# Inputs of a two-layer hybrid trunk stored as columns and tiles, and a bias table stored once per query

## The reference, cut to what matters

```
h = concatenate([meta, x], axis=1)
for layer in range(2):
    nw = norm_w[layer]
    f = swiglu(rms_norm(h, nw[0]), w_gate[layer, 0], w_up[layer, 0], w_down[layer, 0])
    h = h + 0.5 * rms_norm(f, nw[1])
    hn = rms_norm(h, nw[2])
    mix = even_mixer(hn, ...) if layer % 2 == 0 else odd_mixer(hn, ...)
    h = h + rms_norm(mix, nw[3])
    f = swiglu(rms_norm(h, nw[4]), w_gate[layer, 1], w_up[layer, 1], w_down[layer, 1])
    h = h + 0.5 * rms_norm(f, nw[5])
return h[:, 16:]
```

## Time and profile before

| | us |
|---|---|
| median of 3 runs | 2066.17 |
| lowest and highest of them | 2065.93 and 2068.43 |
| the profiled execution, its own time | 2064.44 |
| its span, first to last instruction | 2062.7 |

### The profile page before, as it was taken

How to read it: one execution, slowest core, us unless ns; L and a number is a source line. 1 busy time by engine, 2 the same in 40 slices (tenths; PEclk the granted TensorE clock), 3 DMA queues, 4 the chain that set the end, 5 groups by cost and what they waited for, 6 DMA issues and landing times.

```text
span 2062.7 us, 38830 instructions
## 1 busy us (share of the span) xinstructions
PE 2036.9 (99%) x16054; PEld 1960.1 (95%) x16054; DVE 1381.5 (67%) x2042; ACT 1021.4 (50%) x1751; POOL 102.6 (5%) x97
## 2 busy tenths in 40 slices
PE   8999999999999999999999999999999999999998
PEld 7999999998999999999999999999998789999887
DVE  6989831667485399988228998822663449998723
ACT  5655632446535465556225555622453456555612
POOL 0000000100052200000100000010000020000000
PEclk9999999999999999999999999999999999999999
DMA  4333342321110133333313333331322123333332
GB/s 133 99 103 103 105 127 77 87 73 52 42 32 12 52 103 98 107 105 105 113 50 102 88 107 104 103 112 53 95 81 69 42 67 97 103 109 110 110 96 78
DMA packets 329043, 180.64 MB, mean 88 GB/s; under 512 B 15849, under 2 KB 323344, under 8 KB 328878
## 3 DMA queue, kind: packets, MB, share of 16 engines
q1 hardware_dynamic: 327520, 175.30, 29.6%
q0 software_dynamic: 1024, 2.86, 0.6%
q10 hardware_dynamic: 334, 0.14, 0.0%
HBM read 176.16 MB, written 2.12 MB: 86 GB/s over the span
## 4 chain that ended last, share of the span: by engine, by line
PE 95%; DVE 3%; ACT 1%; DMA 0%; issue 0%; POOL 0%; SPq 0%; DVEq 0%; ACTq 0%
PE psum L1287 35%; PE psum L713 31%; PE psum L725 13%; PE psum L939 5%; PE psum L3172 1%; PE psum L3231 1%; DVE w_hl L569 1%; PE psum L2633 1%; PE psum L3730 1%; PE psum L2645 0%; DMA stage<-ffn_w_gate 0%; PE psum L3746 0%; PE psum L3741 0%; DVE acts L2002 0%; PE psum L816 0%; PE psum L792 0%
## 5 line engine op out<-in xcount | busy, mean ns | idle before, releaser
L1287 PE MATMUL psum<-seven_x,w_hl 128*128 128x264 f32 (+1 forms) x3456 | 438.3, 283 | 0.0
L569 DVE TENSOR_TENSOR w_hl<-stage,w_hl 128x1024 fp32r<-128x1024 f32 (+1 forms) x166 | 220.7, 1330 | 309.7 <-ACT w_hl L562 309.4
L1287 PEld LDWEIGHTS psum<-seven_x,w_hl 128*128 128x128 f32 x3456 | 425.0, 188 | 0.0
L713 PE MATMUL psum<-x_hl,w_hl 128*128 128x264 f32 (+1 forms) x2736 | 368.0, 293 | 2.2 <-DVE w_hl L569 1.9
L713 PEld LDWEIGHTS psum<-x_hl,w_hl 128*128 128x128 f32 x2736 | 348.5, 189 | 14.8 <-issue 5.5
L1287 PE MATMUL psum<-x_hl,w_hl 128*128 128x264 f32 (+1 forms) x2592 | 338.2, 284 | 0.0
L1287 PEld LDWEIGHTS psum<-x_hl,w_hl 128*128 128x128 f32 x2592 | 324.5, 188 | 0.0
L562 ACT ACTIVATE w_hl<-stage 128x1024 fp32r<-128x1024 f32 (+1 forms) x166 | 189.1, 1140 | 227.3 <-PE psum L713 71.5
L713 PE MATMUL psum<-acts,w_hl 128*128 128x264 f32 x2376 | 289.0, 284 | 0.0
L713 PEld LDWEIGHTS psum<-acts,w_hl 128*128 128x128 f32 x2376 | 288.7, 188 | 0.0
L725 PE MATMUL psum<-x_hl,w_hl 128*128 128x264 f32 (+1 forms) x1728 | 219.2, 286 | 0.6 <-DVE w_hl L569 0.4
(11 more groups left out here) (401 smaller groups left out, 2186.5 us busy)
## 6 DMA issues: line engine op xcount, KB each, us to landing
stage<-ffn_w_down SPq DMA_DIRECT2D x48, 704.0 KB, 4.7
stage<-ffn_w_gate SPq DMA_DIRECT2D x52, 512.0 KB, 3.8
stage<-ffn_w_up SPq DMA_DIRECT2D x52, 512.0 KB, 3.8
x_raw<-ffn_w_gate SPq DMA_DIRECT2D x32, 512.0 KB, 3.8
x_raw<-ffn_w_up SPq DMA_DIRECT2D x32, 512.0 KB, 3.8
stage<-odd_w_in SPq DMA_DIRECT2D x24, 512.0 KB, 3.8
stage<-ffn_w_down SPq DMA_DIRECT2D x22, 512.0 KB, 3.5
stage<-even_w_in SPq DMA_DIRECT2D x18, 512.0 KB, 3.8
```

The source lines that it names most:

```text
L569: dve.tensor_tensor(weights(core.w_hl[:, slot.ring, 1, :], *kind), weights(core.stage[:, slot.stage, :], *kind), weights(core.w_hl[:, slot ...
L713: op = pe.matmul(out, lhs, moving[:, moved, kt, t0:t0 + n], start=first and part + moved == 0, stop=last and part == 1)
L1287: op = pe.matmul(k.psum[:, bank, 0:w], k.w_hl[:, slot.ring, side, at:at + P], moving(moved, kt), start=start and kt + side + moved == 0, s ...
```

## The change

Three things are done, all with the layout of what lies in DRAM.

Tokens and channel vectors as columns. The host lays tokens (meta tokens ahead) out as `tokens`, partition by channel tile by token, and the norm weights and channel vectors as `channel_cols`, 128 by 151. SP loads the tokens straight into `h` in four pieces of two channel tiles, in this order: gate tile of group 0, pieces 0 and 1, up tile, pieces 2 and 3. ACT issues two loads, `norm_cols` and `vec_cols`; `ident` goes to POOL's list. All transposes of the start are gone, and with them L1388, L1402 in two pieces, L1410, L2255 and L2257. ACT and DVE start with the weights' split and then take the tokens piece by piece; both wait for both vector loads first.

Bias rows stored once per query. POOL stores `bias_row` 128 times, once for each query row of a block: 1024 pieces of 2800 bytes instead of 8. The read in the even mixer has a stride of one stored copy less one element, gives the queries in their order and lands in `bias`, `bias_near` and `bias_self` themselves. The ten matmuls and ten copies of slot 5 are gone, with the load of `flip`. ACT's wait for the store is gone; `bias_row` now lies where `acts_raw` keeps tile 16, and DVE waits for the store before it writes that tile in the first feed-forward. DVE, not PE, waits for the rows in the even mixer.

Weights by tiles. All weight tiles but those of the last step lie in DRAM in the order in which they land in SBUF, 4 KB (5.5 KB for `ffn_w_down`) in one piece for each partition. The query tiles are gathered on the host and come by one load each.

```diff
-CONST_LOADS = 11
-SCALAR_LOADS = 6
+TOKEN_PIECES = ((0, 1), (2, 3), (4, 5), (6, 7))
+BIAS_TILE = 16
+CONST_LOADS = 8
+SCALAR_LOADS = 2
...
+        self.bias_row = self.at("bias_row", [QH, V_ALL], low + BIAS_TILE * tile)
...
+def load_tokens(core, sp, a, piece):
+    first, last = TOKEN_PIECES[piece][0], TOKEN_PIECES[piece][-1]
+    sp.dma_start(core.h[:, first:last + 1, :], a["tokens"][:, first:last + 1, :])\
+      .then_inc(core.tokens_in[piece], 16)
...
-            src = w[:, n * P:(n + 1) * P].rearrange("(k p) n -> p k n", p=P)
-            sp.dma_start(group_stage(core, n, side, slot), src)\
+            sp.dma_start(group_stage(core, n, side, slot), w[n])\
                 .then_inc(core.w_landed[slot.stage], 16)
+            if phase is core.phases[0] and n == 0:
+                load_tokens(core, sp, a, 2 * side)
+                load_tokens(core, sp, a, 2 * side + 1)
...
+    src = a[name][bass.ds(tile, 1)].rearrange("a p k n -> p (a k) n")
+    sp.dma_start(weights(dst, DT, P), src).then_inc(core.w_landed[slot.stage], 16)
...
+    def run(slot, piece):
+        slot.out_pair = slot.pair
+        if piece == 0:
             pe.wait_ge(k.w_lo, slot.count())
+        for kt in TOKEN_PIECES[piece]:
+            pe.wait_ge(k.x_lo, kt + 1)
+            op = products(k, pe, phase, slot, kt, kt, k.x_hl, kt == 0, kt == DT - 1)
         if kt == DT - 1:
             op.then_inc(k.slot_used, 1)
...
+    run(slots[0], 0)
     pe.wait_ge(k.consts_set, 5)
     pe.wait_ge(k.consts_in, 16 * (CONST_LOADS - SCALAR_LOADS))
...
+    run(slots[0], 1)
+    run(slots[1], 0)
+    run(slots[1], 1)
+    for piece in (2, 3):
+        for slot in slots:
+            run(slot, piece)
...
+    def piece(i):
+        act.wait_ge(k.tokens_in[i], 16)
+        for kt in TOKEN_PIECES[i]:
+            col = first.before.pre_col + kt
+            act.activation(k.x_hl[:, 0, kt, :], k.h[:, kt, :], ACT.Copy, scale=k.norm_cols[:, col:col + 1])\
+               .then_inc(k.x_hi, 1)
+        for kt in TOKEN_PIECES[i]:
+            act.activation(k.in_squares[:, kt, :], k.h[:, kt, :], ACT.Square).then_inc(k.sq_made, 1)
...
+    high(0)
+    act.wait_ge(k.norms_in, 16)
+    act.wait_ge(k.vectors_in, 16)
+    piece(0)
+    piece(1)
+    high(1)
+    piece(2)
+    piece(3)
+    high(2)
...
-    act.wait_ge(k.bias_stored, 16)
...
+    if phase is k.phases[0] and n == BIAS_TILE:
+        dve.wait_ge(k.bias_stored, 16)
...
+    low(0)
+    dve.wait_ge(k.norms_in, 16)
+    dve.wait_ge(k.vectors_in, 16)
+    piece(0)
+    piece(1)
+    low(1)
+    piece(2)
+    piece(3)
+    dve.wait_ge(k.sq_made, DT)
+    add_squares(DT // 2)
+    low(2)
...
-    pool.wait_ge(k.cols_ready, 4)
-    pool.dma_start(a["bias_scratch"], k.bias_row[0:QH, :]).then_inc(k.bias_stored, 16)
+    pool.wait_ge(k.cols_ready, 2)
+    copies = k.bias_row[0:QH, :].unsqueeze(1).broadcast_to([QH, P, V_ALL])
+    pool.dma_start(a["bias_scratch"].rearrange("p h v -> h p v"), copies).then_inc(k.bias_stored, 16)
...
-        return bass.AP(tensor, first, [[1, rows], [V_ALL, QH], [1, n]])
+        return bass.AP(tensor, first + rows - 1, [[QH * V_ALL - 1, rows], [V_ALL, QH], [1, n]])
...
+    pool.dma_start(e.bias[:, :, META:BANDS], skewed(V_BAND, P, 2 * P)).then_inc(e.rows_in, 16)
...
-        pe.wait_ge(e.rows_in, 80)
-        for j in range(BIAS_FLIPS):
-            if j >= len(FLIP_BANKS):
-                pe.wait_ge(e.bias_set, j - len(FLIP_BANKS) + 1)
...
-        pe.wait_ge(e.bias_set, BIAS_FLIPS)
         pe.wait_ge(e.v_rows_set, 3)
...
-        for j in range(BIAS_FLIPS):
-            bank = FLIP_BANKS[j % len(FLIP_BANKS)]
-            dve.wait_ge(e.bias_flip, j + 1)
...
+        dve.wait_ge(e.rows_in, 64)
         dve.memset(e.gates[:], 1.0).then_inc(e.gates_clear, 1)
```

More of the change, by code:

```diff
@@ L233, in count @@
             before["added"] += phase.early if self.split else DT - 1
-        if not self.split:
-            before["h"] += 2 * DT
         if self.pre_col is not None:
@@ L316, in linked @@
 def linked(steps):
-    queries = [s.slot0 for k, s in steps if k == "dense" and s.kind == "in" and s.layer == 0]
-    twice = [first + t for first in queries for t in range(QH // KVH)]
     for at, (kind, step) in enumerate(steps):
@@ L523, in landed @@
         first = self.base + RING * (self.i if self.peeled else 1)
-        twice = [g for g in self.twice if g <= first and g % 2 == self.stage]
-        return self.i * (16 * RING // 2) + 16 * (self.base // 2 + 1 + len(twice) - self.single)
+        return self.i * (16 * RING // 2) + 16 * (self.base // 2 + 1 - self.single)
 def walk(core, phase, engine, step, ahead=0, between=None, late=False):
@@ L674, in load_slot @@
     if phase.kind == "rows":
-        rows = a["ffn_w_down"][phase.layer, phase.ffn][bass.ds(slot.local * P, P), :]
+        rows = a["ffn_w_down_rows"][bass.ds(slot.local * P, P), :]
         sp.dma_start(dst[:, 0:D], rows).then_inc(core.w_landed[slot.stage], 16)
@@ L1039, in tensor_input @@
               stop=True).then_inc(k.cols_flip, 1)
-    for slot in slots:
-        run(slot, DT - 2)
-        run(slot, DT - 1)
+    run(slots[0], 1)
[4 more added lines that the diff above has]
+            run(slot, piece)
 def tensor_dense(core, pe, phase):
@@ L3957, in odd_vector, with tiles_of @@
         lo(kt)
+def tiles_of(array, count):
+    rows, cols = array.shape[-2], count * P
+    tiles = array[..., 0:cols].reshape(array.shape[:-2] + (rows // P, P, count, P))
+    return np.moveaxis(tiles, -2, -4).swapaxes(-3, -2)
 def laid_out(name, array):
+    if name == "ffn_w_gate" or name == "ffn_w_up":
+        return tiles_of(np.asarray(array), FT)
+    if name == "ffn_w_down":
+        tiles = tiles_of(np.asarray(array), DT)
+        tiles = tiles.reshape(tiles.shape[:-2] + (2, FH, P))
+        return np.moveaxis(tiles, -3, -4)
+    if name == "even_w_in":
+        whole = np.array(array[0])
+        heads = whole[:, 0:QH * HD].reshape(D, KVH, GRP, HD).transpose(0, 2, 1, 3)
+        whole[:, 0:QH * HD] = heads.reshape(D, QH * HD)
+        return tiles_of(whole, EVEN_TILES)
+    if name == "odd_w_in":
+        return tiles_of(np.asarray(array)[0], ODD_TILES)
+    if name == "odd_w_out":
+        return tiles_of(np.asarray(array)[0], DT)
     if name == "rel_bias_table" or name == "swa_sinks":
```

226 lines of the change are left out of this document (55 added, 171 removed).

## The result

The changed kernel takes 2085.09 us (median of 4 runs, 2085.00 to 2085.86); the kernel before, beside it, takes 2066.05. The ratio is 1.0094, with an interval from 1.0081 to 1.0106: slower by 19 us, where 13 us less were forecast. The profiled execution's span is 2084.1 us instead of 2062.7.

The account below looks back on a forecast made before the run. PE, busy 2036.9 of 2062.7 us, bounds the kernel; 9.3 us at the start plus 3.7 in slot 5, with 0 for weights and store, take 13.0 off 2066.17: 2053.2 us, range 2049.5 to 2059.

Parts of the forecast that it names:

- the room that the store takes on the DMA engines: Head, between 19 and 40 us: the store runs beside four to five weight tile loads; cost 0, upper bound 4 us.
- Rival (3): Head, 19 to 60 us: the store crowds out weight loads, giving back 4 us: 2057.2 us; chance 12%.
- The rule on the number of engines: Store of the bias rows: 8 DMA engines by the rule, some 15 us at half of peak, weight tiles waiting on these.
- The start: First two slots' 96 products: their end moves from 32.8 to 23.5 us, a gain of 9.3 us.
- S: Start: the moment when the first tokens can be scaled, taken as 6.5 us, range 5.9 to 8.
- 4.7 us after its first product: Start: PE works at half rate for about 4.7 us after its first product, charged as 2.35 us.
- The opposite reading: Start: slow time runs from PE's first instruction, lasts 10 us and costs 2.7 us more.
- the second rival: Start brings only half: vectors land at 7.9 us, slow stretch lasts 10 us; 2057.4 us; chance 15%.
- Slot 5: Even mixer's input projection: PE no longer waits for DVE's copies before the next score product; gain 3.7 us.
- The clock in the mixer: Two windows of 50 us from 500 us on: 3 us of work lost, other spacing may lose 1.5 more or less.
- The weights by tiles: Weight loads in pieces of 4 KB instead of 512 bytes: worth 0, bounds 0 and -0.5 us.
- rival (5): Wait before tile 16: a slow store holds DVE and PE; 68 us lost, 2121 us, at the upper bound; chance 2%.

Follow-up runs that it names:

- e13: Changed kernel, but the store reads 8 partitions of `h` lying 4 apart, 128 times each (bias values wrong): 2055.32 us.
- e4: Changed kernel with the bias rows stored once to DRAM, then copied 128 times within DRAM (the two-step kernel): 2050.35 us, ratio 0.9939 to the kernel before.
- e1: Changed kernel with the old bias path (one small store, ten matmuls and ten copies in slot 5): 2052.14 us, ratio 0.9949 to the kernel before.
- e5: e4 with the weights in DRAM in rows as the reference has them, query tiles still gathered on the host: 2053.92 us.
- e6: e4 with 26 matmuls of ones by ones into an unused PSUM bank ahead of PE's first product: 2049.54 us.
- e9: Changed kernel, but the store reads 8 partitions of `h` lying 2 apart, 128 times each (bias values wrong): 2060.75 us, timed once.
- e11: e4's text unchanged, timed again in more rounds against the kernel before: 2053.59 us, ratio 0.9951.
- e7: Changed kernel, but the store reads 16 neighbouring partitions of `h`, 64 times each (bias values wrong): 2063.78 us.

## Why the prediction was wrong, point by point

**The store of the bias rows: its length was mis-sized.** The prediction took 21 us for it, from a read by the same queue, with 7.4 and 243 us as bounds; it took 61.3. The bounds held it. At 21 us it would have cost nothing (e13's 20.1). The nearest row was the wrong relative: that read lands in 128 partitions, and the limit is on the side that has 8. It still is no limit where the side of few partitions isn't SBUF: e4's copy reads 8 rows in DRAM and takes 13.7 us.

**Its price, the step that failed and turned the sign.** The term is the room that the store takes on the DMA engines: "I take 0, with 4 us as the upper bound". It measured 30.8 us in the head, about 23 of idle time and 7 of lower clock after it; without the big store (e1) it is 0. The 4 had no working behind it, and the lower clock after a long wait was no term at all. Rival (3) had the place and the mechanism right (low parts late between 30 and 80 us) and the size wrong by eight times. What could have been worked out from the rows shown: PE eats a gate and an up tile in 96 x 0.123 = 11.8 us, two stage buffers let two loads run at a time, so a pair of loads that takes longer than that sets PE's pace. While the store ran each of four loads took 24 to 30 us, and the second pair landed 26 us behind the first. The range of the store's length (7.4 to 243 us) times such a loss would have given an upper bound of tens of us, not 4. The runs give the price by the store's length: 0 at up to 20 us, 3.6 to 9.4 us at 31 to 33, 30.8 at 61.3 and 42 at 118 (the head alone).

**The rule on the number of engines** (the Trainium skill, DMA: Bandwidth & Descriptors, section on why a DMA increments its semaphore by 16) was right on the count: the share is 0.5 while the store runs. The 15 us that the prediction drew from it were a quarter of the truth, since these 8 engines read over two ways out of SBUF.

**The start: right in its steps, off by the slow stretch.** The timeline of the changed kernel, answering to the earlier trace rows:

```profile
6.72 1.36 ACT L1333 ACTIVATE x_hl<-h,norm_cols 128x528 fp32r<-128x528 f32 x2 [0.91 <-DMA vec_cols<-channel_cols]
...
8.51 2.98 PE L691 MATMUL psum<-x_hl,w_hl 128*128 128x264 f32 x12 [8.51 <-DVE x_hl L2196]
...
31.14 1.05 PE L1269 MATMUL psum<-sq_sum,ones 128*128 128x264 f32 x4
```

S is 6.7 us where 6.5 was taken, and the vectors decide it, as one of the two candidates; PE starts at 8.51 instead of 8.05. The token sum was forecast near 28: it stands at 31.14 here, at 27.6 to 28.3 in e1, e4, e5, e6 and e9, and at 28.6 to 32.2 in the other eight traces. The difference is the step "4.7 us after its first product": in the changed kernel products run at half rate until about 19 us. The window from 16 to 20 us in the changed kernel, then in e4:

```profile
16.00:20.00 4.00, 4.00 (x23) 4.00 (x22) 3.40 (x3) 3.98 (x8) 0.07 (x1) 1.00 0.25 102
```

```profile
16.00:20.00 4.00, 4.00 (x35) 4.00 (x34) 3.59 (x3) 3.98 (x8) 0.26 (x1) 1.00 0.20 83
```

23 products against 35 in the same window, at a granted clock that reads 1.00 in both. "The opposite reading", 10 us of slow time, which the second rival held, is what the changed kernel's execution did; in e1 and e4 the stretch was shorter than forecast, over within 3.4 us of the first product. Both happen with the same text: e4 and e11 are one kernel, and e11's lasts until about 16.6. So the gain of the start is 9.5 us in some executions and 5 to 7 in others (e4; e7, the changed kernel, e11), all against the one traced execution of the kernel before, and what decides it is open. Three small slips of the working change nothing: 3 + 1.1 / 0.39 is 5.8, PE reaches the bias matmuls at 8.05 + 12 x 0.246 = 11.0 and not 11.4, and the last channel tile is wanted after 78 products, not 84.

**Slot 5: right at its place.** The forecast was 3.7 us, the next score product 0.9 us after the transposes' end, released by ACT's copy of the values' rows. The changed kernel, answering to the earlier trace rows:

```profile
447.62 0.71 PE L2543 MATMUL psum<-ident,even_proj 128*16 128x128 f32 x5 [0.80 <-DVE even_proj L1871]
...
448.92 0.25 ACT L2662 ACTIVATE v_rows<-psum 128x128 f32<-128x128 f32 x1
...
449.22 0.61 PE L2598 MATMUL psum<-even_proj 64*16 64x16 f32 x8 [0.88 <-ACT v_rows L2662]
449.76 6.45 PE L691 MATMUL psum<-x_hl,w_hl 128*128 128x264 f32 x40
```

The idle time is 0.88 us and its releaser the one named. From the transposes to the score product it is 1.60 us, where it was 427.42 - 422.12 = 5.30: 3.70 us.

**The clock in the mixer: right as a term of the range, too narrow in size.** In this execution it fell just behind slot 5 (48 products in 7.4 us at 449.8) and once more at 579.7, where before it fell near 524 and at 558: the 0.97 of the earlier trace rows in other places. The forecast had 3 us, 1.5 more or less; the traces have from nothing (e1, e4) to 6.2 us (e5's four stretches).

**The weights by tiles: right**, 0.2 us at the start. The loads into `stage` went from 3.8 to 3.6 us, those into `x_raw` from 3.8 to 4.2, and outside of the store PE lost nothing by either.

**DVE's wait at group 16, rival (5): it doesn't decide**, as forecast; the store landed at 81 us, and DVE comes to that group at 229. The price of the slow store was paid between 39 and 93 us, where nobody waits for its semaphore at all.

With the store out of the way the sum holds: 13.0 us were forecast, and the two-step kernel is 13.8 and 10.5 us below the kernel before in its two sets of runs. Some of that is luck, since the slow stretch at the start and the clock in the mixer each move it by some us either way.

## What to carry to other kernels

A transfer that nobody waits for can still have a price: what it takes from the loads beside it, for as long as it runs. Work out its length from where in SBUF it reads (how many partitions, and how many groups of four), not from its bytes alone, and compare the loads' time while it runs with the time in which PE eats what they bring. Here a row in SBUF that is to be written many times was better stored to DRAM once and copied there.

## What the runs showed of the hardware

A store out of few SBUF partitions, each read many times in pieces of 2800 bytes, is limited by their place: 24 GB/s out of four neighbours, 47 out of eight, 93 out of sixteen or of eight that lie 2 apart, 86 out of eight that lie 16 apart, 143 out of eight that lie 4 apart. A load of 512 KB into all 128 partitions, 3.6 us as the median of its kind, takes 24 to 30 us beside such a store from eight neighbours, with half of the DMA engines' time free (share 0.52).

TensorE's granted clock, 1.00 while it was fed, read 0.50 in the windows from 44 to 48 and from 68 to 72 us of the changed kernel, in which it stood idle for a load, and the 96 products that came next at 48.3 took 14.57 us instead of 11.84.

At the start of an execution PE can work at half rate while the granted clock reads 1.00; the stretch ended before 11.9 us in e4 and behind 16 us in e11, two executions of the same text.
